# Two halves of the second MLP layer, laid between the strips of the first

## The chip, the cores and the metric

The kernel runs on one core of a Trainium2 chip. The metric is the device time of one execution in microseconds (us), as a median of runs. Before the change it is 2875.54 us over 3 runs (2875.34 to 2878.55).

## The reference

One layer of a hybrid encoder on 2048 prompt tokens and 64 sample tokens of width 1024: a normalised input projection into four head groups (one of them stick-breaking attention), an output projection, then an MLP of width 4096. Only the last part is touched:

```
x = x + g1 * mix
h2 = rmsnorm(x, ln2_g) * (1.0 + sc2) + sh2
x = x + g2 * (jnp.square(jax.nn.relu(h2 @ mlp_w1)) @ mlp_w2)
```

All of it is float32. The kernel splits each operand of a product into a high part, as TensorE's reduced float32 holds it, and a low remainder, and adds three products: high by high, low weight by high, high weight by low.

## The kernel before, in words

Everything that is transposed lies with features in the 128 partitions and tokens along the row. The last phase, `tail_phase`, takes the tokens in 4 blocks: 512 tokens in blocks 0 to 2, and 576 in block 3 (512 and the 64 sample tokens), which are done as two groups of 256 and 320 columns. For each block it does the output projection (`out`, 8 tiles) and a sum for the norm (`nsum`), and then the MLP in 16 chunks of 256 hidden features.

One chunk has two **strips** of the first layer (`hid`, ft = 0 and 1; 128 hidden features each). A strip is one accumulation of 24 matmuls (8 pieces of 128 input features, three products each; lines 2224, 2225, 2228). ScalarE reads the strip's PSUM bank (relu, L1890) and squares it into `g_hi` (L1892), VectorE squares it too and takes the remainder `g_lo` (L2075, L2077). Behind the strips of chunk c come the 8 **projection tiles** of chunk c-1 (`prj`, d = 0 to 7; lines 2266 to 2268): each multiplies both 128-feature parts of the preceding chunk's `g` by second-layer weights in 6 matmuls, and VectorE adds the tile into the residual `xs` (L2043). Chunk 0 has no projection tiles; the last two chunks of a block are projected together, later (`prj2`).

**Banks.** All these tiles use four PSUM banks in turn, `dn[u % 4]` for tile number u. TensorE waits in `bank(u)` until tile u-4 has been read out, by ScalarE for a strip and by VectorE for a projection tile.

**One order for all.** `walk` is a generator of the order of tiles. Each engine's program is written by one run of `walk` with its own callbacks, so all engines have the same order, and each engine's queue is strictly in that order. The order of weight loads comes from it too: `next_loads` says which weight strips are loaded behind which tile. Within a chunk these are four: the first-layer strips `w1` of the next chunk, one behind each `hid`, and the second-layer strips `w2` of this chunk, in a ring of four buffers, behind `prj` d = 3 and d = 7. Call them A and B (`w1`), C and D (`w2`). At chunk 0 there are no projection tiles, and the two `w2` strips are loaded behind the two `hid` tiles, behind A and behind B.

**What one load does.** In `load_for` SyncE's queue issues the load of the low part from a scratch in HBM (`load_lo`, L1629, blocks 1 to 3 only), then the load of the raw weights three places further on (`load_weights`, L1613 and L1616), for which it waits until ScalarE has converted the strip in hand (the raw buffers are three). ScalarE converts raw weights to the high part (`weights_hi`, L1756). In block 0 VectorE makes the low part (`weights_lo`, L1946), and it is stored to the scratch. A projection tile with d = 0 waits for both low parts of its `w2` (`lo_ready`).

**Attention in slots.** The attention of later blocks runs between these tiles. A strip takes 4 slots, a projection tile 1, so a chunk takes 16. Attention pair t starts at a fixed slot, `PRO + 43 * i // 4`, so a new pair comes every 10 or 11 slots. Its steps hang on that start: scores on TensorE, two sigmoids on ScalarE two slots later, VectorE's `scan` five slots later (two scans L1960, a copy, a product L1965), transposes and copies from 10 to 13, products with the values at 14 and 15. Each engine does the steps that are due before it goes on with its next tile, in its own queue.

In chunk 4 of blocks 1 to 3, `yt` puts one transposed output tile of the preceding block behind each projection tile; ScalarE copies it out (L1924). In chunk 1 GpSimd adds squares for the final norm (L1742), and in chunk 3 VectorE scales the finished block beside its other work.

Of the kernel before, what the change touches and what calls it, by code (L numbers as in the profile page):

```python
# [14 lines left out]
KT = D_MODEL // P  # L15
# [1280 lines left out]
def tail_phase(nc, const, x_v, o_v, q_v, k_v, sbv_p, sbv_s, cache_sb_v, w_out, mlp_w1, mlp_w2, y_prompt, y_sample):  # L1296
# [5 lines left out]
    NC = D_FF // P // 2  # L1302
# [4 lines left out]
    def groups(b):  # L1307

        return [(0, BLK)] if b < NB - 1 else [(0, HALF), (HALF, TMAX)]
# [43 lines left out]
    def walk(out, nsum, hid, prj, prj2, fsum, yt):  # L1353

        def opening(b):
            for f in range(KT):
                for g in range(len(groups(b))):
                    out(b, f, g)

        def sums(b):  # L1360
            for g in range(len(groups(b))):
                nsum(b, g)

        opening(0)
        sums(0)
        for b in range(NB):
            for c in range(NC):
                for ft in range(2):
                    for g in range(len(groups(b))):
                        hid(b, c, ft, g)  # L1370
                for d in range(KT if 1 <= c < NC - 1 else 0):
                    for g in range(len(groups(b))):
                        prj(b, c - 1, d, g)
                    if c == 4 and b:
                        yt(b - 1, d // 2, d % 2)
                if c == 2 and b:
                    fsum(b - 1, 0)
            if b + 1 < NB:
                opening(b + 1)
                for d in range(KT):  # L1380
                    prj2(b, d, 0)
                    if d == 0:
                        sums(b + 1)
        for g in range(len(groups(NB - 1))):
            for d in range(KT):
                prj2(NB - 1, d, g)
            for i in range(2 if g else 0):
                for v in range(2):
                    yt(NB - 1, i, v)
            fsum(NB - 1, g)  # L1390
        for i in range(2, TPB + 1):
            for v in range(2):
                yt(NB - 1, i, v)
# [7 lines left out]
    def count(kind, slots, by):  # L1401
        def one(*key):
# [10 lines left out]
        return one  # L1413

    walk(count("out", 4, PV), count("nsum", 0, PA), count("hid", 4, PA), count("prj", 1, PV), count("prj2", 2, PV),
         count("fsum", 0, PA), count("yt", 0, PA))
    for b in range(1, NB):
# [12 lines left out]
    def next_loads(kind, b, *key):  # L1430

        if kind == "start":
            return [("wo", 0, 0), ("wo", 0, 1)]
        if kind == "out":
            f = key[0]
            return [("wo", b, f + 2)] if f + 2 < KT else [("w1", b, 0, f + 2 - KT)]
        if kind == "hid":
            c, ft = key
            then = [("w1", b, c + 1, ft)] if c + 1 < NC else [("wo", b + 1, ft)] if b + 1 < NB else []
            return then + ([("w2", b, c, ft)] if c in (0, NC - 1) else [])  # L1440
        if kind == "prj":
            c, d = key
            return [("w2", b, c + 1, d // 4)] if d % 4 == 3 else []
        return []

    ring_no = {}
# [1 line left out]
    def count_loads(kind):  # L1448
        def one(b, *key):
            if key and key[-1] != last_group(b):  # L1450
                return
            for w in next_loads(kind, b, *key[:-1]):
                load_no[w] = len(load_no)
                ring = "w2" if w[0] == "w2" else "w1"
                ring_no[w] = sum((x[0] == "w2") == (ring == "w2") for x in load_no) - 1
        return one
# [3 lines left out]

    count_loads("start")(0)
    walk(count_loads("out"), nothing, count_loads("hid"), count_loads("prj"), nothing, nothing, nothing)
    load_list = list(load_no)
    ring_list = {False: [w for w in load_list if w[0] != "w2"], True: [w for w in load_list if w[0] == "w2"]}
# [56 lines left out]
    with ExitStack() as ctx:  # L1521
# [81 lines left out]
        def _(sp):  # L1603
# [85 lines left out]
            def load_for(kind):  # L1689
                def one(b, *key):  # L1690
                    u = tile_no[(kind, b, *key)]
                    slots.upto(slot_end[u])
                    if key[-1] != last_group(b):
                        return
                    for w in next_loads(kind, b, *key[:-1]):
                        if w[1]:
                            load_lo(w)
                        if load_no[w] + 3 < len(load_list):
                            load_weights(load_list[load_no[w] + 3])
                        if w[1] == 0:  # L1700
                            store_lo(w)
                    if kind == "hid" and key[0] == NC - 3 and key[1] == 0 and b + 1 < NB:
                        for i in range(6):
                            load_strip(b + 1, i)
                    if kind == "prj" and key[0] == 5 and key[1] == KT - 1 and 1 <= b and b + 1 < NB:
                        load_x(b + 1)
                return one
# [19 lines left out]
            for w in next_loads("start", 0):  # L1727
                load_weights(load_list[load_no[w] + 3])
                store_lo(w)
            walk(load_for("out"), nothing, load_for("hid"), load_for("prj"), nothing, nothing, store_rows)  # L1730
            for i in range(2):
                sp.wait_ge(y_out[i], 16 * (len(yt_no) // 2))
# [607 lines left out]
```

How the kernel before makes its waits and increments, by code:

```python
def wait(eng, sem, value):  # L57
    if not (isinstance(value, int) and value <= 0):
        eng.wait_ge(sem, value)
# [11 lines left out]
    def link(self, ins):  # L72
        self.n += 1
        ins.then_inc(self.sem, 1)
        self.eng.wait_ge(self.sem, self.base + self.n)
# [110 lines left out]
        @block.sync  # L186
# [16 lines left out]
            for c in range(1, NCH, 2):  # L203
                load_wada(sp, c)
                if c == 1:
                    load_rows(rows2, parts2, rows_in[1])
                    sp.dma_start(lra_raw[:, :].rearrange("p (k n) -> p k n", n=RANK),
                                 w_in[0].rearrange("(k p) n -> p k n", p=P)[:, :, OFF_LRA:OFF_LRA + RANK]
                                 ).then_inc(lra_in, 16)
                    for i in range(2):
                        sp.dma_start(mixc["wa2"][RANK * i:RANK * i + RANK, :], gla_wa2[0]).then_inc(blocks_in, 16)
                    sp.wait_ge(zeroed, 1)
                    for n in range(4):
                        for g, w in enumerate((rg_wa, rg_wx)):
                            sp.dma_start(mixc["rgw"][64 * (n % 2):64 * (n % 2) + 64, g, n // 2,
# [1 line left out]
                if c == 7:  # L218
                    for by in ("act", "dve"):
                        sp.wait_ge(tb_free[by], max(n for f in range(KT) for w, n in [turn_freed[turn_no["raw", f]]] if w == by))
                    sp.wait_ge(tb_free["act"], turn_freed[turn_no["raws", 0]][1])
# [2 lines left out]
            sp.wait_ge(blocks_in, 16 * 10)
            sp.wait_ge(raw_stored, 32)
```

## Time and profile before

| what | value |
|---|---|
| median of 3 runs | 2875.54 us (2875.34 to 2878.55) |
| profiled execution | 2876.38 us, its span 2874.6 us |
| granted TensorE clock, mean | 0.978 |
| TensorE matmul busy | 2744.9 us, 95% of the span |
| VectorE busy | 1466.1 us, 51% |
| ScalarE busy | 1273.9 us, 44% |
| DMA | 447.21 MB, mean 156 GB/s |

The span is the time from the first to the last instruction; the profiled execution's own time is 1.8 us longer. Times in rows are counted from the span's start. The `tail_phase` matmuls begin at about 768 us; block 0's output projection begins at 835 us, and the MLP strips of block 3 begin after 2420 us.

### The profile page before, as it was taken

The page shows a single profiled execution, that of the slowest core. Times are in us where ns is not written, and L with a number is a line of the kernel's source. Part 1 is how long each engine was busy: PE and PEld are TensorE (multiplying, and loading weights), DVE is VectorE, ACT ScalarE, POOL GpSimd, SP SyncE. Part 2 cuts the span into 40 slices and gives each one's busy share as a digit, 9 for nine tenths or more (in the row PEclk, how much of TensorE's full clock was granted, in tenths as well). Part 3 has the DMA queues.
Part 4 walks back from the last instruction along what each step waited for, and adds up shares of the span by engine and source line. Part 5 has one row for each costly group of instructions (what it writes and reads, how often), then busy time and mean ns, then how long its engine had stood idle before and what let it go on. Part 6 is the DMA issues. An engine that isn't in the chain of part 4 may idle for free.

```text
span 2874.6 us, 36899 instructions
## 1 busy us (share of the span) xinstructions
PE 2744.9 (95%) x14665; PEld 2243.1 (78%) x14665; DVE 1466.1 (51%) x2333; ACT 1273.9 (44%) x1949; POOL 35.1 (1%) x43
## 2 busy tenths in 40 slices
PE   7999999999878999999999999999999999999997
PEld 2589777777656777777877877777777789999996
DVE  4544554645335656575546455544555444545544
ACT  3375737455445343434444434445433443332233
POOL 0000000000000000000010000001000000100000
PEclk9999999999869999999999999999999999999999
DMA  9533353333524455555356555535555463555551
GB/s 328 174 103 111 103 160 110 111 114 91 192 81 156 148 150 164 162 176 187 118 166 196 175 162 187 183 95 176 183 187 161 154 226 117 194 163 165 176 166 51
DMA packets 381505, 447.21 MB, mean 156 GB/s; under 512 B 18716, under 2 KB 288983, under 8 KB 381335
## 3 DMA queue, kind: packets, MB, share of 16 engines
q1 hardware_dynamic: 375094, 432.26, 47.4%
q10 hardware_dynamic: 6240, 12.58, 1.2%
q8 instruction: 118, 1.93, 0.3%
q14 instruction: 53, 0.43, 0.0%
HBM read 374.00 MB, written 70.79 MB: 155 GB/s over the span
## 4 chain that ended last, share of the span: by engine, by line
PE 64%; DVE 4%; ACT 3%; DMA 1%; issue 1%; SPq 0%; DVEq 0%; ACTq 0%
PE t_dn L2224 11%; PE t_dn L2228 10%; PE t_dn L2225 10%; PE t_dn L2266 7%; PE t_dn L2268 6%; PE t_dn L2267 6%; PE t_ob L2170 4%; PE t_sc L2147 3%; PE t_wt L2159 2%; DVE t_left L1960 1%; PE t_dn L2289 1%; PE t_dn L2291 1%; PE t_dn L2290 1%; PE t_sc L2151 1%; DVE t_xs L2043 1%
## 5 line engine op out<-in xcount | busy, mean ns | idle before, releaser
L2224 PE MATMUL t_dn<-t_h_hi,t_w1h 128*128 128x512 f32 (+2 forms) x1600 | 589.2, 368 | 7.6 <-ACT t_h_hi L1872 3.1
L2043 DVE SCALAR_TENSOR_TENSOR t_xs<-t_dn,modT,t_xs 128x512 f32<-128x512 f32 (+2 forms) x768 | 422.7, 580 | 322.7 <-PE t_dn L2268 172.5
L2228 PE MATMUL t_dn<-t_h_lo,t_w1h 128*128 128x512 f32 (+2 forms) x1600 | 570.0, 356 | 2.3 <-DVE t_h_lo L2025 2.1
L2225 PE MATMUL t_dn<-t_h_hi,t_w1l 128*128 128x512 f32 (+2 forms) x1600 | 567.9, 355 | 0.0
L2266 PE MATMUL t_dn<-t_g_hi,t_w2h 128*128 128x512 f32 (+2 forms) x1120 | 412.4, 368 | 17.5 <-DVE t_xs L2043 15.3
L2268 PE MATMUL t_dn<-t_g_lo,t_w2h 128*128 128x512 f32 (+2 forms) x1120 | 397.6, 355 | 0.0
L2267 PE MATMUL t_dn<-t_g_hi,t_w2l 128*128 128x512 f32 (+2 forms) x1120 | 396.5, 354 | 0.0
L2075 DVE TENSOR_TENSOR t_rt<-t_rt 128x512 f32<-128x512 f32 (+2 forms) x160 | 95.9, 599 | 552.9 <-ACT t_g_hi L1892 552.9
L2224 PEld LDWEIGHTS t_dn<-t_h_hi,t_w1h 128*128 128x128 f32 x1600 | 305.2, 191 | 63.4 <-issue 27.4
L2228 PEld LDWEIGHTS t_dn<-t_h_lo,t_w1h 128*128 128x128 f32 x1600 | 304.1, 190 | 44.3 <-DVE t_h_lo L2025 3.2
L1890 ACT ACTIVATE t_rt<-t_dn 128x512 f32<-128x512 f32 (+2 forms) x160 | 83.7, 523 | 563.6 <-PE t_dn L2228 563.5
L2225 PEld LDWEIGHTS t_dn<-t_h_hi,t_w1l 128*128 128x128 f32 x1600 | 305.3, 191 | 31.7 <-issue 0.7
L1267 PE MATMUL f_zr<-hn_hi,f_w_hi 128*128 128x512 f32 (+1 forms) x880 | 321.4, 365 | 7.4 <-ACT f_gb L810 2.6
L1269 PE MATMUL f_zr<-hn_hi,f_w_lo 128*128 128x512 f32 (+1 forms) x880 | 314.0, 357 | 0.0
L1268 PE MATMUL f_zr<-hn_lo,f_w_hi 128*128 128x512 f32 (+1 forms) x880 | 312.7, 355 | 0.0
L2266 PEld LDWEIGHTS t_dn<-t_g_hi,t_w2h 128*128 128x128 f32 x1120 | 212.4, 190 | 60.4 <-DVE t_xs L2043 27.2
L1772 ACT ACTIVATE t_aT<-t_wt 128x512 f32<-128x512 f32 (+4 forms) x168 | 86.9, 517 | 368.4 <-PE t_wt L2159 368.3
L2268 PEld LDWEIGHTS t_dn<-t_g_lo,t_w2h 128*128 128x128 f32 x1120 | 212.1, 189 | 28.2
L2267 PEld LDWEIGHTS t_dn<-t_g_hi,t_w2l 128*128 128x128 f32 x1120 | 212.6, 190 | 21.0
L968 DVE TENSOR_TENSOR f_w_lo<-f_wraw,f_w_hi 128x1024 fp32r<-128x1024 f32 x88 | 107.7, 1224 | 214.3 <-ACT f_w_hi L777 214.1
L1960 DVE TENSOR_TENSOR_SCAN t_left<-t_left 128x512 f32<-128x512 f32 (+5 forms) x168 | 180.5, 1116 | 43.2 <-ACT t_taken L1765 40.6
L777 ACT ACTIVATE f_w_hi<-f_wraw 128x1024 fp32r<-128x1024 f32 x88 | 92.8, 1054 | 244.9 <-PE f_zr L1269 220.3
(312 smaller groups left out, 3662.8 us busy)
## 6 DMA issues: line engine op xcount, KB each, us to landing
t_raw<-in_mlp_w_dram SPq DMA_DIRECT2D x256, 512.0 KB, 4.5
t_w1l<-lo_scratch SPq DMA_DIRECT2D x120, 512.0 KB, 3.5
t_w2l<-lo_scratch SPq DMA_DIRECT2D x96, 512.0 KB, 5.6
f_wraw<-in_w_in_dram SPq DMA_DIRECT2D x88, 512.0 KB, 3.9
lo_scratch<-t_w1l SPq DMA_DIRECT2D x40, 512.0 KB, 5.3
t_raw<-in_w_out_dram SPq DMA_DIRECT2D x32, 512.0 KB, 5.1
lo_scratch<-t_w2l SPq DMA_DIRECT2D x32, 512.0 KB, 5.4
wada<-in_w_ada_dram ACTq DMA_DIRECT2D x6, 2048.0 KB, 12.6
```

Source lines behind the costliest of these rows:

```text
L1267: pe.matmul(out, wh, hi, start=(k == 0), stop=False)
L1268: pe.matmul(out, wh, lo, start=False, stop=False)
L1269: ins = pe.matmul(out, wl, hi, start=False, stop=(k == KT - 1))
L1960: ins = dve.tensor_tensor_scan(keep[:, j, ::-1], keep[:, j, ::-1], keep[:, j, ::-1], upto[:, j:j + 1], ALU.mult, ALU.min)
L2043: ins = dve.scalar_tensor_tensor(out=cols, in0=dn[u % 4][:, s - a:t - a], scalar=modT[:, mod + f, m:m + 1], in1=cols, op0=ALU.mult, op1=AL ...
L2170: ins = pe.matmul(ob[0:p.rows, at_col:at_col + HD], aT[0:p.kr, j, v * p.rows:(v + 1) * p.rows], vp[p.piece % 2][0:p.kr, v, HD * j:HD * j + ...
L2224: pe.matmul(out, hi[:, k, :], h_hi[:, k, a:e], start=(i == 0), stop=False)
L2225: pe.matmul(out, lo[:, k, :], h_hi[:, k, a:e], start=False, stop=False)
L2228: ins = pe.matmul(out, hi[:, k, :], h_lo[:, k, a:e], start=False, stop=(i == KT - 1))
L2266: pe.matmul(out[:, 0:e - a], hi[:, d, :], g_hi[c % 2][:, ft, a:e], start=(ft == 0), stop=False)
L2267: pe.matmul(out[:, 0:e - a], lo[:, d, :], g_hi[c % 2][:, ft, a:e], start=False, stop=False)
L2268: ins = pe.matmul(out[:, 0:e - a], hi[:, d, :], g_lo[c % 2][:, ft, a:e], start=False, stop=(ft == 1))
```

## The change

The 8 projection tiles no longer follow both strips: tiles d = 0 to 3 follow the first strip and tiles d = 4 to 7 the second. The loads of the two `w2` strips both come behind tile d = 7.

```
                 for ft in range(2):
                     for g in range(len(groups(b))):
                         hid(b, c, ft, g)
-                for d in range(KT if 1 <= c < NC - 1 else 0):
-                    for g in range(len(groups(b))):
-                        prj(b, c - 1, d, g)
-                    if c == 4 and b:
-                        yt(b - 1, d // 2, d % 2)
+                    for d in range(4 * ft, 4 * ft + 4 if 1 <= c < NC - 1 else 0):
+                        for g in range(len(groups(b))):
+                            prj(b, c - 1, d, g)
+                        if c == 4 and b:
+                            yt(b - 1, d // 2, d % 2)
...
         if kind == "prj":
             c, d = key
-            return [("w2", b, c + 1, d // 4)] if d % 4 == 3 else []
+            return [("w2", b, c + 1, ft) for ft in range(2)] if d == KT - 1 else []
```

In `next_loads`, c is the chunk that is projected, so c + 1 is the chunk in whose place the tile stands. A, B, C, D keep their order.

## Rows read from the trace of the kernel before

**Rows 1.** The page, part 1: engine, busy us, share of the span, instructions.
```profile
PE 2744.9 (95%) x14665; PEld 2243.1 (78%) x14665; DVE 1466.1 (51%) x2333; ACT 1273.9 (44%) x1949; POOL 35.1 (1%) x43
```

**Rows 2.** Waits of TensorE: who waited for whom, total us, times, longest.
```profile
PE t_dn L2266 <- DVE t_xs L2043: 15.3, 10, 2.4
...
PE t_dn L2266 <- ACT t_yrow L1924: 2.1, 1, 2.1
...
PE t_dn L2224 <- DVE t_xs L2043: 1.5, 1, 1.5
```

**Rows 3.** Timeline of VectorE, block 0, chunk 3: start, us, instruction, idle before it.
```profile
992.67 0.69 DVE L2075 TENSOR_TENSOR t_rt<-t_rt 128x512 f32<-128x512 f32 x1 [5.58 <-ACT t_g_hi L1892]
...
994.00 1.22 DVE L1946 TENSOR_TENSOR t_w1l<-t_raw,t_w1h 128x1024 fp32r<-128x1024 f32 x1
...
995.34 2.46 DVE L1960 TENSOR_TENSOR_SCAN t_left<-t_left 128x512 f32<-128x512 f32 x2
...
999.04 2.72 DVE L2043 SCALAR_TENSOR_TENSOR t_xs<-t_dn,modT,t_xs 128x512 f32<-128x512 f32 x4
```

**Rows 4.** Timeline of TensorE, block 0: chunk 3, first and fifth projection tile; chunk 13.
```profile
991.99 0.48 PE L2266 MATMUL t_dn<-t_g_hi,t_w2h 128*128 128x512 f32 x1
...
999.84 0.50 PE L2266 MATMUL t_dn<-t_g_hi,t_w2h 128*128 128x512 f32 x1 [2.16 <-DVE t_xs L2043]
...
1285.77 0.50 PE L2266 MATMUL t_dn<-t_g_hi,t_w2h 128*128 128x512 f32 x1 [0.55 <-DVE t_xs L2043]
```

**Rows 5.** Windows behind three stalls: engines' busy us (instructions), then clock, DMA share, GB/s.
```profile
940.50:943.90 3.40, 3.40 (x10) 2.65 (x9) 3.32 (x5) 0.00 (x0) 0.00 (x0) 0.51 0.69 240
1000.00:1003.40 3.40, 3.40 (x18) 2.81 (x19) 3.40 (x5) 0.07 (x1) 0.00 (x0) 1.00 0.08 28
1459.40:1462.80 3.40, 3.40 (x10) 2.53 (x9) 1.58 (x3) 1.52 (x3) 3.11 (x3) 0.50 0.37 112
```

**Rows 6.** Timelines of SyncE, chunk 0 of blocks 1 to 3: the second w2 low load.
```profile
1436.19 0.38 SPq L1629 DMA_DIRECT2D t_w2l<-lo_scratch  x1
...
1950.90 0.58 SPq L1629 DMA_DIRECT2D t_w2l<-lo_scratch  x1
...
2442.42 0.74 SPq L1629 DMA_DIRECT2D t_w2l<-lo_scratch  x1
```

**Rows 7.** DMA issues in those three instants: KB each, us from issue to landing.
```profile
t_w2l<-lo_scratch SPq DMA_DIRECT2D x1, 512.0 KB, 5.7
...
t_w2l<-lo_scratch SPq DMA_DIRECT2D x1, 512.0 KB, 5.3
...
t_w2l<-lo_scratch SPq DMA_DIRECT2D x1, 512.0 KB, 6.4
```

**Rows 8.** Timeline of TensorE, chunk 1 of blocks 1 to 3: around the second strip's start.
```profile
1438.34 0.39 PE L2228 MATMUL t_dn<-t_h_lo,t_w1h 128*128 128x512 f32 x1
1438.57 0.39 PE L2224 MATMUL t_dn<-t_h_hi,t_w1h 128*128 128x512 f32 x1
...
1953.98 0.39 PE L2224 MATMUL t_dn<-t_h_hi,t_w1h 128*128 128x512 f32 x1
...
2446.28 0.28 PE L2224 MATMUL t_dn<-t_h_hi,t_w1h 128*128 128x256 f32 x1
```

**Rows 9.** Timelines of VectorE and GpSimd in block 2, chunk 1.
```profile
1968.39 3.84 DVE L1960 TENSOR_TENSOR_SCAN t_left<-t_left 128x384 f32<-128x384 f32 x2
...
1965.37 11.40 POOL L1742 TENSOR_TENSOR t_st<-t_st 128x512 f32<-128x512 f32 x7 [502.36 <-ACT t_st L1831]
```

**Rows 10.** Block 3, chunk 7: first projection tile on TensorE, D's low load on SyncE; chunk 8.
```profile
2614.85 0.28 PE L2266 MATMUL t_dn<-t_g_hi,t_w2h 128*128 128x256 f32 x1
...
2618.76 1.35 SPq L1629 DMA_DIRECT2D t_w2l<-lo_scratch  x1
...
2640.45 0.28 PE L2266 MATMUL t_dn<-t_g_hi,t_w2h 128*128 128x256 f32 x1
```

**Rows 11.** DMA issues of that low load: KB each, us from issue to landing.
```profile
t_w2l<-lo_scratch SPq DMA_DIRECT2D x1, 512.0 KB, 7.1
```

## The prediction

> **What bounds the kernel now.** Part 1 of the page comes first: TensorE's matmuls are busy 95% of the span, every other engine about half [rows 1]. Nothing can be gained on another engine; what an order of tiles can move is TensorE's idle time, so the second view is TensorE's waits. Of those that hang on this order there are three [rows 2]: 15.3 us in 10 waits of projection tiles for VectorE's addition L2043 (a PSUM bank not yet read out), 1.5 us of one strip for the same, 2.1 us for ScalarE's copy of an output tile. The third view, the timelines around one such wait, shows how it arises. In chunk 3 of block 0 the second strip ends just before the first projection tile at 991.99 [rows 4]. VectorE works in its order: square and remainder of the strip from 992.67, a weight remainder at 994.00, then the attention scan that was due, from 995.34, and only at 999.04 the first tile's addition [rows 3]. The fifth tile needs that bank and starts at 999.84, printed as 2.16 us idle [rows 4]. The scan blocks 999.04 - 995.34 = 3.7 us.
>
> I counted from the code where scans fall in a chunk's 16 slots (0 to 3 and 4 to 7 the strips, 8 to 15 the tiles). A scan due in slot 8 or 9, right behind the strip, belongs to 8 of the 10 waits: block 0, chunks 1, 3, 5, 7 (slot 8), 11, 13 (slot 9), and block 2, chunks 8 and 10 (slot 8). The smallest is 0.55 us, in chunk 13 [rows 4]. Two more are in block 1, chunks 1 and 3, at slot 10 with GpSimd's or final-norm work beside it. The strip's 1.5 us is block 2, chunk 1, slot 12. A scan in a strip's slots runs beneath that strip and costs nothing.
>
> **Removed.** The waits printed are 15.3 + 1.5 + 2.1 = 18.9 us. A printed gap begins where the preceding matmul's modelled end is (0.39 us), while matmuls start 0.23 us apart [rows 8]; so each of the 12 is short by 0.16, and TensorE loses 18.9 + 12 x 0.16 = 20.8 us. Some stalls cost more: the granted clock behind the one at 940 was 0.51 for 3.4 us with 10 matmuls in it, behind the equally long one at 999.84 it was 1.00 with 18 [rows 5]. Of the five stalls of 2 us and more on this list three are followed by 3.4 us at the lower of the two clocks (1.2 instead of 2.4 GHz), which costs half of it, 1.7 us: 5.1 us. Together 25.9 us. In the new order scans of slots 8 to 11 lie beneath the second strip, so the slot-8 to slot-10 waits go. The copy of output tiles gets a strip's pause after four tiles, so its 2.1 us goes too; should that one stay, 2.3 + 1.7 us are lost again. What is late next are the two terms below.
>
> **Added 1: second-layer weights at chunk 1.** A projection tile needs both low parts of its weights. For chunk 0 the second is issued behind B, at 1436.19, 1950.90 and 2442.42 in blocks 1, 2 and 3 [rows 6], and takes 5.7, 5.3 and 6.4 us [rows 7]: landed at 1441.9, 1956.2, 2448.8. Before, two strips of chunk 1 cover this. Now the first projection tile stands where the second strip started, at 1438.57, 1953.98 and 2446.28 [rows 8], and everything up to there is as before. TensorE waits 3.3 + 2.2 + 2.5 = 8.0 us. Queued behind it on TensorE are the whole chunk and the attention steps. I take 8.0; it is below that only if landings get shorter (0 at 2.4 to 3.9 us), above if longer. In block 0 VectorE makes this remainder just in time, and I count 0.
>
> **Added 2: scans behind the new bursts.** A burst is now four tiles and then a strip. Only its first tile's bank comes due four tiles later with no strip in between (the next strip takes it); the banks of the other three come due behind that strip. So a scan in slots 5 or 13, where four and six of them fall now, costs nothing, and one in slots 4 or 12 costs what slot 8 cost. Four fall there: block 0, chunks 12 and 14 (slot 4), in the same place against the strip as the 999.84 case: 2.16 + 0.16 = 2.3 each [rows 4], 4.6. Block 2, chunks 1 and 3 (slot 12). In chunk 1 the scan meets GpSimd's adds: 3.84 us for two scans of 384 columns, while 7 adds fill 11.4 us beside it [rows 9], against 2.46 for two of 512 [rows 3]. Without GpSimd I put this stall at 0.7, with it at 2.8, and take 2.8, since four of the adds still follow the strip. Chunk 3 has value products on TensorE in between: 0.4. One scan in block 1, chunk 4, slot 5, lies in the burst with output tiles, where banks turn over twice as fast: 0.4. Sum 8.2; bounds 0 and 5 x 2.8 = 14.
>
> The GPSIMD Engine Reference of the Trainium skill (its table of specifications) says that GpSimd shares its SBUF interfaces with VectorE and contends with VectorE instructions that have two SBUF inputs, as the scan has. The trace's longer scan agrees; by that rule the 2.8 holds, without it the sum is 2.1 us lower.
>
> **Added 3: C and D in all other chunks.** Moving C to tile d = 7 moves four things: ScalarE's conversion of C now stands behind all attention steps up to slot 15; on SyncE the low load of C, then a raw load that waits for that conversion, then D's low load; in block 0 VectorE does both remainders in a row. From the end of the second strip to the tile that needs them there were 8 tiles and 2 strips, 2640.45 - 2614.85 = 25.6 us in block 3 [rows 10]; now 4 tiles and 1 strip, 12.8. D's low load was issued 2618.76 - 2614.85 = 3.9 us behind that strip [rows 10], as ScalarE does B, C, D in a row, and took 7.1 [rows 11]: 11.0, with 1.8 to spare. In blocks 1 and 2 attention lengthens both sides: where no step of ScalarE stands in slots 12 to 15 it is much the same; where one or two stand there the load goes out up to 4 us later, with a shorter queue of DMAs and more attention on TensorE, and I get between 0 and 1 us to spare. Late by my count are block 2, chunk 4 (about 1.3, output copies on ScalarE) and block 1, chunk 7 (about 1.7, an attention head's roots there). Bounds 0 and 0.5 us in each of 39 chunks, 20. I take half of 3.0 and 0.7 for the rest, 2.2, nearest to rows 10 and 11.
>
> **Added 4: the lower clock.** Of the new stalls six are over 2 us (three of added 1, two of block 0, one of block 2). At three in five and 1.7 us [rows 5]: 6.1; bounds 0 and 10.2.
>
> **Sum.** No instruction is added or taken away. Added 8.0 + 8.2 + 2.2 + 6.1 = 24.5, removed 25.9: -1.4 us. Against the profiled execution, 2876.4 us (span 2874.6 and 1.8 around it), that is 2875.0; the runs' median, 2875.5, is 0.9 lower, so 2874.1. I predict 2874.
>
> **Rivals.**
> *The bursts win (faster).* Shorter bursts let VectorE recover and the small terms vanish: added 1 stays (8.0), of added 2 the two in block 0 (4.6), added 3 is 0, the clock falls twice (3.4). 16.0 against 25.9: -9.9, so 2866. For it: the spare 1.8 us in block 3, and slots 5 and 13 free. Against it: the two scans with GpSimd and output tiles beside them. Chance 0.28.
>
> *Weights late in every chunk (slower).* D's low part becomes the bound in place of VectorE: its spare time is 1.8 us in block 3 and less elsewhere, so it decides from a landing of about 8.9 us, or an issue 1.8 us later. At 0.5 us in 39 chunks added 3 is 19.5 in place of 2.2, and the time is 2874 + 17 = 2891; at a third of the chunks 2880. For it: every low load stands behind a raw load and ScalarE's conversion. Against: in block 3 nothing but these weights uses ScalarE there. Chance 0.20, with what the clock may add.
>
> *It doesn't do what it says: a wait moves one tile on.* Scans behind the first strip stall as those behind the second did, and the removed 20.8 us comes back nearly whole in the second strips' bank waits: 8.0 more than before with added 1, 2883. Against it: the count of slots, four in place of eleven. It is part of the slower chance.
>
> **How the numbers follow.** 0.2% is 5.7 us, about what a measurement of this kernel can tell from no change. My case has 0.52 and falls within it; faster 0.28, slower 0.20. The range takes in the faster rival's 2866 and of the slower one the third of the chunks with some clock, 2886; my case's own range is 2870 to 2880.
>
> **What would show it.** Right: no waits of L2266 for VectorE in block 0 before chunk 12; one wait of L2266 for the DMA into `t_w2l` in chunk 1 of blocks 1, 2 and 3, of 2 to 3.5 us; strips L2224 waiting for L2043 in block 0, chunks 12 and 14; busy times as before. Wrong: waits for `t_w2l` in many chunks (the slower rival), or waits of strips for L2043 all over (the third); a time below 2868 with added 1 in the trace would mean that added 2 and 4 were too large.

## The result, and the profile after

The changed kernel takes 2885.23 us (median of 15 runs, 2881.99 to 2889.81); the kernel before, in turn with it, 2876.83 us (15 runs, 2871.84 to 2879.56). The ratio is 1.0029, with a 95% interval of 1.0021 to 1.0037: 8.4 us slower. The forecast was 2874, no change. The profiled execution of the changed kernel took 2888.46 us, 3.2 us more than its median; what follows is read from that one execution.

The page, part 1, of the changed kernel. It answers to [rows 1]; the span grew from 2874.6 to 2886.6 us.

```profile
span 2886.6 us, 36897 instructions
...
PE 2752.2 (95%) x14665; PEld 2249.4 (78%) x14665; DVE 1459.1 (51%) x2333; ACT 1274.3 (44%) x1949; POOL 33.2 (1%) x43
```

The instruction counts agree with those of before, so the difference is in waits and in the clock. Of the 12.0 us between the two spans 3.8 are there before the first MLP strip (it starts at 900.44 instead of 896.68 us), in code that the change doesn't touch; in the other kernels' traces it starts anywhere from 895.2 to 900.8 us. The other 8.2 us come behind it. That this is almost what lies between the medians is chance in part, for these are two single executions.

TensorE's waits after (who waited for whom, total us, times, longest) answer to [rows 2]:

```profile
PE t_dn L2266 <- DMA t_w2l<-lo_scratch: 16.2, 8, 4.6
...
PE t_dn L2224 <- DVE t_xs L2043: 7.9, 3, 3.6
...
PE t_dn L2224 <- DMA t_w1l<-lo_scratch: 3.1, 1, 3.1
...
PE t_dn L2266 <- DVE t_xs L2043: 0.8, 1, 0.8
```

The bank waits of projection tiles fell from 15.3 us in 10 to 0.8 in one. In their place stand 16.2 us in 8 waits for the low part of second-layer weights, which did not exist before. The single waits, from TensorE's timeline (start, us, instruction, idle before it):

```profile
1239.33 0.50 PE L2224 MATMUL t_dn<-t_h_hi,t_w1h 128*128 128x512 f32 x1 [2.16 <-DVE t_xs L2043]
...
1297.52 0.50 PE L2224 MATMUL t_dn<-t_h_hi,t_w1h 128*128 128x512 f32 x1 [2.16 <-DVE t_xs L2043]
...
1438.61 0.77 PE L2266 MATMUL t_dn<-t_g_hi,t_w2h 128*128 128x512 f32 x1 [4.62 <-DMA t_w2l<-lo_scratch]
...
1558.96 0.47 PE L2266 MATMUL t_dn<-t_g_hi,t_w2h 128*128 128x512 f32 x1 [1.10 <-DMA t_w2l<-lo_scratch]
...
1644.93 0.47 PE L2266 MATMUL t_dn<-t_g_hi,t_w2h 128*128 128x512 f32 x1 [0.96 <-DMA t_w2l<-lo_scratch]
...
1957.36 0.47 PE L2266 MATMUL t_dn<-t_g_hi,t_w2h 128*128 128x512 f32 x1 [2.40 <-DMA t_w2l<-lo_scratch]
...
1980.55 0.80 PE L2224 MATMUL t_dn<-t_h_hi,t_w1h 128*128 128x512 f32 x1 [3.61 <-DVE t_xs L2043]
...
2455.32 0.56 PE L2266 MATMUL t_dn<-t_g_hi,t_w2h 128*128 128x256 f32 x1 [3.70 <-DMA t_w2l<-lo_scratch]
...
2567.73 0.36 PE L2266 MATMUL t_dn<-t_g_hi,t_w2h 128*128 128x256 f32 x1 [2.07 <-DMA t_w2l<-lo_scratch]
```

The first two are block 0, chunks 12 and 14; the tiles at 1438.61, 1957.36 and 2455.32 are chunk 1 of blocks 1, 2 and 3; that at 1980.55 is the strip behind chunk 1's second burst; those at 1558.96 and 2567.73 are chunk 5, and 1644.93 is chunk 8. Two shorter ones for these weights (0.46 and 0.87 us) are in block 2, chunks 7 and 12; the tile of chunk 5 there waits 0.77 us, which the profile puts down to ScalarE (L1890).

The second `w2` low load of chunk 0, on SyncE's timeline in blocks 1 to 3 [rows 6], and its time from issue to landing (last number of the second list) [rows 7]:

```profile
1431.46 0.38 SPq L1629 DMA_DIRECT2D t_w2l<-lo_scratch  x1
...
1951.72 0.58 SPq L1629 DMA_DIRECT2D t_w2l<-lo_scratch  x1
...
2447.59 0.77 SPq L1629 DMA_DIRECT2D t_w2l<-lo_scratch  x1
```

```profile
t_w2l<-lo_scratch SPq DMA_DIRECT2D x1, 512.0 KB, 7.0
...
t_w2l<-lo_scratch SPq DMA_DIRECT2D x1, 512.0 KB, 5.5
...
t_w2l<-lo_scratch SPq DMA_DIRECT2D x1, 512.0 KB, 7.6
```

1431.46 + 7.0 = 1438.5, and the tile starts at 1438.61: TensorE waits for this landing and nothing else.

Windows behind four of the stalls, with columns as in [rows 5] (busy us and instructions of each engine, granted clock, DMA share, GB/s):

```profile
1438.70:1442.10 3.40, 3.40 (x10) 2.71 (x11) 0.48 (x1) 0.00 (x0) 0.00 (x0) 0.50 0.28 111
...
1980.60:1984.00 3.40, 3.40 (x8) 2.72 (x9) 1.87 (x3) 0.00 (x0) 0.36 (x1) 0.50 0.70 275
2455.40:2458.80 3.40, 3.40 (x15) 3.40 (x16) 0.71 (x2) 0.63 (x1) 3.07 (x3) 0.50 0.36 145
...
1297.60:1301.00 3.40, 3.40 (x17) 2.85 (x18) 1.84 (x3) 0.00 (x0) 0.00 (x0) 1.00 0.04 14
```

The three stalls over 3.5 us bring a stretch at 1.2 GHz (0.50), with 8 to 15 matmuls in these windows; that of 2.16 us before 1297.52 does not (1.00), nor do the others of this list, of 2.07, 2.16 and 2.40.

**The ledger.** I read off TensorE's timelines when each chunk starts in both traces, and took the steps of the difference (us). Where one chunk has several causes (block 1, chunk 1, say), its step is divided by the printed waits, 0.16 us added to each as in the prediction, and what remains is put down to the clock; so the sum is measured, its division in those chunks is a reckoning.

| term | predicted | found |
|---|---|---|
| removed, clock with it | -25.9 | -31.8 |
| added 1, weights at chunk 1 | 8.0 | 11.2 (4.8, 2.6, 3.9) |
| added 2, scans and output tiles | 8.2 | 10.1 |
| added 3, weights in other chunks | 2.2 | 9.0 |
| added 4, lower clock | 6.1 | 7.9 |
| block 1's first output tile | not named | 2.5 |
| last projection at the lower clock | not named | 1.5 |
| rest | 0 | -2.2 |
| sum | -1.4 | 8.2 |

### The profile page after: what moved, and what is told of

It is laid out like the page before. It is cut to its first block, busy times and chain, and to the rows that moved or that the text cites. A ratio compares the mean times of both kernels' runs of the same rounds, so it can differ in the third digit from the quotient of the medians.

```text
span 2886.6 us, 36897 instructions
## 1 busy us (share of the span) xinstructions
PE 2752.2 (95%) x14665; PEld 2249.4 (78%) x14665; DVE 1459.1 (51%) x2333; ACT 1274.3 (44%) x1949; POOL 33.2 (1%) x43
## 4 chain that ended last, share of the span: by engine, by line
PE 64%; DVE 3%; DMA 3%; ACT 2%; issue 1%; SPq 0%; DVEq 0%; ACTq 0%
PE t_dn L2224 10%; PE t_dn L2228 10%; PE t_dn L2225 10%; PE t_dn L2266 7%; PE t_dn L2268 7%; PE t_dn L2267 7%; PE t_ob L2170 4%; PE t_sc L2147 3%; PE t_wt L2159 2%; DMA t_w2l<-lo_scratch 2%; PE t_dn L2289 1%; PE t_dn L2291 1%; PE t_dn L2290 1%; PE t_sc L2151 1%; DVE t_left L1960 1%
## 5 line engine op out<-in xcount | busy, mean ns | idle before, releaser
L2266 PE MATMUL t_dn<-t_g_hi,t_w2h 128*128 128x512 f32 (+2 forms) x1120 | 412.2, 368 | 18.5 <-DMA t_w2l<-lo_scratch 16.2
L1890 ACT ACTIVATE t_rt<-t_dn 128x512 f32<-128x512 f32 (+2 forms) x160 | 83.7, 523 | 618.3 <-PE t_dn L2228 618.3
```

What stands on the lines that cost most here:

```text
L2266: pe.matmul(out[:, 0:e - a], hi[:, d, :], g_hi[c % 2][:, ft, a:e], start=(ft == 0), stop=False)
```

## The experiments

Two theories stood against each other. **Weights**: the order of tiles itself gains, and the loss is the low loads of `w2`, whose cover the new order halved. **Order**: the short bursts lose as much in bank waits and clock as the long ones did, and if the weights came earlier, other waits would take their place. In the diffs, lines with - are those of the changed kernel; the labels e1 to e10 are those that the expectations use. Line numbers in the profiles of these kernels are up to six higher than in the changed kernel. Where a kernel ran once, its time alone settles little (the kernel before ranged over 7.6 us in 11 runs beside these), and the waits and chunk lengths of its trace have to decide.

**Chunk 1 alone back (e1).** In chunk 1 of blocks 1 to 3 both strips run ahead of the 8 tiles again, with C and D at d = 3 and d = 7 there.

```
-                    for d in range(4 * ft, 4 * ft + 4 if 1 <= c < NC - 1 else 0):
+                    tiles = range(4 * ft, 4 * ft + 4) if split(b, c) else range(KT if ft else 0)
+                    for d in tiles if 1 <= c < NC - 1 else ():
```
with `split(b, c)` false for b > 0 and c = 1, and in `next_loads`, for a chunk that isn't split, the order of before.

> The changed kernel, but chunk 1 of blocks 1, 2 and 3 keeps the order of before (both strips, then eight tiles, C behind d = 3). Theory 'weights': the loss sits at chunk 1, where the first projection tile waits for the second low part of w2. In the trace of after, chunk 1 of blocks 1 to 3 and the slow clock behind it lengthen the way by 3.1, 7.4 and 6.4 us, 16.9 in all; undone, the time falls from 2885 to about 2868, and the waits of L2266 for the DMA into t_w2l in chunk 1 are gone. Rival 'bursts': the loss is in VectorE's scans behind the short bursts of all chunks; then little comes back, 2880 to 2885.

Measured: 2869.56 us (8 runs), ratio to before 0.9978 (0.9968 to 0.9988). The three chunks 1, of 56 chunks with projection tiles, carry the whole loss and more: without them the change is faster than the kernel before.

**The second w2 load of chunk 0 earlier (e2).** All tiles stay; the load goes ahead of B, one strip earlier.

```
+            if b and c == 0:
+                return then + [("w2", b, 0, i) for i in range(0 if ft else 2)]
             return then + ([("w2", b, c, ft)] if c in (0, NC - 1) else [])
```

> The changed kernel, but in chunk 0 of blocks 1 to 3 both w2 strips are loaded behind the first strip, ahead of B, instead of one behind each strip. The order of tiles is that of after. Theory 'weights': the three waits at chunk 1 (4.8, 2.6 and 3.9 us over the usual pitch in the trace of after) and the slow clock behind two of them (some 4.6 us) go, 15.8 in all: about 2869; the strip behind chunk 1 of block 2 still waits 3.8 for VectorE. Rival 'bursts': VectorE's waits take their place as soon as TensorE is no longer held there: 2880 to 2885.

Measured: 2870.36 us (9 runs), ratio 0.9975 (0.9965 to 0.9984). TensorE's waits in this kernel:

```profile
PE t_dn L2226 <- DVE t_xs L2045: 7.9, 3, 3.6
...
PE t_dn L2268 <- DMA t_w2l<-lo_scratch: 6.3, 4, 2.4
```

The waits for `t_w2l` fell by 16.2 - 6.3 = 9.9 us, and two of the three stalls that brought the lower clock went. These are about 9.9 + 2 x 2.5 = 14.9 us, as much as the medians differ (2885.23 - 2870.36 = 14.9). The agreement to a tenth is luck: the stall of 2.43 us in block 3, chunk 5, brought a stretch at 1.2 GHz here (0.50 from 2547.60 to 2550.90), and that of 2.07 us in the changed kernel did not. The bank waits did not grow. So the order of tiles need not be undone: an earlier load does the same.

**One half of the blocks each (e3, e4).** `split` is `b == 0` in the first kernel and `b > 0` in the second.

> The new order in block 0 alone, blocks 1 to 3 in the order of before (loads too). In block 0 VectorE makes the low parts and no load of them exists. Theory 'weights': block 0 keeps its gain, 11.1 us from the first strip to chunk 15 in the trace of after, less 2.5 at the first output tile of block 1, which waits for its low part there: 2877 - 8.5 = 2868. Rival 'bursts': short bursts cost in every block, so 2877 or more.

> The new order in blocks 1 to 3 alone, block 0 in the order of before. Theory 'weights': all the loss is here: from the start of block 1 to the end the trace of after is 16.7 us longer than that of before, so 2877 + 17 = 2894. Rival 'a loss spread over all blocks': no more than 2885.

Measured: block 0 alone 2868.27 us (6 runs), ratio 0.9972 (0.9960 to 0.9984); blocks 1 to 3 alone 2892.12 us (5 runs), ratio 1.0056 (1.0044 to 1.0069). The two differences to before, -8.4 and +15.4, add up to +7.0, near the change's +8.4. In block 0 the low weights are made on VectorE and don't come by DMA, and there the order gains; in blocks 1 to 3 they come by DMA, and there it loses. The list of waits of the second kernel has:

```profile
PE t_dn L2272 <- DMA t_w2l<-lo_scratch: 15.3, 9, 4.1
```

**The loads' move alone (e5).** All tiles in the order of before, C and D both behind d = 7 (`split` always false); one run.

> The order of tiles of before, with only the change of loads: C and D both behind tile d = 7. Theory 'weights': the move costs only when one strip, not two, covers it; here two do, so every chunk of blocks 1 to 3 takes what it takes in before, within 0.3 us, and the sum is within 2 us of before. Rival 'loads': moving C costs by itself; then waits for t_w2l in chunks 5 and 8 of blocks 1 to 3, as in after, some 8 us.

Measured: 2874.82 us, span 2873.0. With 8 tiles and 2 strips to cover them, no projection tile waits for `t_w2l`, and chunks 1 to 14 of blocks 1 and 2 agree with before within 0.3 us. Block 3 doesn't, against the expectation: its chunks 4 and 5 are 3.24 and 0.69 us shorter, for ScalarE's copy (L1924) is gone though no tile has moved. In block 0 chunk 4 is 1.37 us longer, and chunks 9 and 10 are 2.14 and 1.50 us shorter, as attention's wait of 1.85 us at the end of chunk 9 and the stretch at the lower clock behind it are gone. So 5.2 us of what the ledger calls removed (2.61, 1.13 and 1.46 in those chunks) come with the loads' move alone too; the tiles' order without it gives as much (2.66, 1.82 and 1.46 in e6, below), so either is enough. And block 1 begins 2.75 us later, for its first output tile waits for its own weights:

```profile
1335.08 0.47 PE L2228 MATMUL t_dn<-t_h_hi,t_w1h 128*128 128x512 f32 x1 [2.78 <-DMA t_w1l<-lo_scratch]
```

In the kernel before this wait was 0.95 us. Both low parts of chunk 14's `w2` in block 0 are now stored back to back (issued at 1317.40 and 1318.59 in the changed kernel), and block 1's first low load waits for all stores of weights loaded before its own. The second of them took 7.55 us and landed 13.5 us after chunk 15 began; in the kernel before it was stored alone, took 5.63 us and landed after 10.5. The price at block 1's start was 2.3 to 3.1 us in each of the eight kernels that load C and D together in block 0, and 0.0 to 0.1 in the three that do not.

**C back at d = 3 (e6).** The tiles of the changed kernel; one run.

```
-            return [("w2", b, c + 1, ft) for ft in range(2)] if d == KT - 1 else []
+            return [("w2", b, c + 1, d // 4)] if d % 4 == 3 else []
```

> The tile order of after, but C is loaded behind tile d = 3 as before (so ahead of B), D behind d = 7. Theory 'weights': D's low load is issued at once behind B, not behind the conversion of C, so the waits for t_w2l in chunks 5, 7 and 8 (about 8 us with the slow clock) fall to under 3; the three at chunk 1 stay, 8 to 11 us, for the loads of chunk 0 are the same. Rival 'order of tiles': they stay as in after.

Measured: 2877.96 us, span 2876.1. TensorE's waits for the weights:

```profile
PE t_dn L2266 <- DMA t_w2l<-lo_scratch: 9.4, 3, 4.0
```

All three are chunk 1. Chunk 5, whose weights are loaded among the output tiles of chunk 4, lost 1.34, 1.05 and 2.3 us in blocks 1 to 3 of the changed kernel and none here; chunk 8 of block 1 0.46 instead of 2.64. So 8.5 of the ledger's 9.0 us for added 3 came from C's place.

**GpSimd's adds made small (e7).** In chunk 1 GpSimd adds 16 of 512 columns of the squares; the rest of the final norm's sum is left out. One run.

```
-                pool.tensor_tensor(nacc[:, 0:n], nacc[:, 0:n], st[f % 2][:, 0:n], ALU.add).then_inc(n_acc, 1)
+                pool.tensor_tensor(nacc[:, 0:16], nacc[:, 0:16], st[f % 2][:, 0:16], ALU.add).then_inc(n_acc, 1)
```

> The changed kernel, but GpSimd's adds of squares in chunk 1 of blocks 1 to 3 take 16 columns instead of all (the rest of the sum for the final norm is left out). Theory 'GpSimd slows the scan': in block 2, chunk 1, the two scans of 384 columns fall from about 3.8 us to 1.9, the strip behind them waits under 2 us instead of 3.8, and the slow clock behind it goes: chunks 1 and 2 of block 2 shorter by 4 to 5 us. Rival 'the scan's place alone': unchanged.

Measured: 2879.73 us. Timelines of VectorE and GpSimd in block 2, chunk 1, first of the changed kernel, then of this one:

```profile
1973.85 4.04 DVE L1960 TENSOR_TENSOR_SCAN t_left<-t_left 128x384 f32<-128x384 f32 x2
...
1973.88 7.08 POOL L1742 TENSOR_TENSOR t_st<-t_st 128x512 f32<-128x512 f32 x4 [9.65 <-ACT t_st L1831]
```

```profile
1969.92 1.98 DVE L1960 TENSOR_TENSOR_SCAN t_left<-t_left 128x384 f32<-128x384 f32 x2
...
1970.48 1.43 POOL L1742 TENSOR_TENSOR t_st<-t_st 128x16 f32<-128x16 f32 x2 [0.30 <-ACT t_st L1831]
```

The same two scans take half as long when the adds beside them are short, and the strip behind them waits 0.67 us instead of 3.61:

```profile
1973.68 0.50 PE L2224 MATMUL t_dn<-t_h_hi,t_w1h 128*128 128x512 f32 x1 [0.67 <-DVE t_xs L2043]
```

The stretch at the lower clock behind that strip is gone. Chunks 1 and 2 of block 2 together cost 4.2 us less than in the changed kernel, although the wait of 2.15 us for the weights in chunk 1 brought such a stretch here (0.50 from 1953.30 to 1956.60).

**Every w2 pair early (e8).** Both `w2` strips of a chunk of blocks 1 to 3 are loaded behind that chunk's first strip, a whole chunk ahead of use.

```
+            if b and c < NC - 1:
+                return then + [("w2", b, c, i) for i in range(0 if ft else 2)]
...
-            return [("w2", b, c + 1, ft) for ft in range(2)] if d == KT - 1 else []
+            return [("w2", b, c + 1, ft) for ft in range(2)] if d == KT - 1 and not b else []
```

> The changed kernel, but in blocks 1 to 3 both w2 strips of every chunk (C and D) are loaded behind the first strip, behind A and ahead of B, instead of behind tile d = 7. Block 0 and the order of tiles as in after. Theory 'weights': the waits left in e2 for the DMA into t_w2l (6.3 us in 4 places, chunks 5, 7 and 8, with the slow clock some 8) go too, because D's low load is no longer queued on SyncE behind ScalarE's conversion of C and the attention steps before it: 2870 - 8 = 2862, and no wait of L2266 for t_w2l is left. Rival 'ScalarE': three conversions in a row behind the first strip delay ScalarE's relu and copies, and other waits take their place: 2870 or more.

Measured: 2867.99 us (6 runs), ratio 0.9967 (0.9955 to 0.9979). All waits for `t_w2l` by DMA are gone, but it is 6 us above what Weights expected. In block 3, chunk 4, a new wait of 5.0 us came, and this chunk is 3.73 us longer than before instead of 2.61 shorter, which is the 6 us. TensorE, ScalarE and SyncE there:

```profile
2525.47 0.38 PE L2226 MATMUL t_dn<-t_h_hi,t_w1h 128*128 128x256 f32 x1 [5.03 <-ACT t_yrow L1926]
```
```profile
2524.82 1.21 ACT L1926 ACTIVATE t_yrow<-t_dn 128x512 f32<-128x512 f32 x2 [8.27 <-DMA out_dram<-t_yrow]
```
```profile
2513.72 0.38 SPq L1618 DMA_DIRECT2D t_raw<-in_mlp_w_dram  x1
2514.15 0.58 SPq L1631 DMA_DIRECT2D t_w2l<-lo_scratch  x1
2514.77 0.44 SPq L1618 DMA_DIRECT2D t_raw<-in_mlp_w_dram  x1
2515.26 1.56 SPq L1631 DMA_DIRECT2D t_w2l<-lo_scratch  x1
2516.86 0.43 SPq L1615 DMA_DIRECT2D t_raw<-in_mlp_w_dram  x1
2517.34 9.05 SPq L1717 DMA_DIRECT2D out_dram<-t_yrow  x4
```

The stores of output rows stand behind the bunched weight loads on SyncE; ScalarE waits for them to land before it overwrites the row buffer, and TensorE for ScalarE. Here Order was right, in this one place.

**Both mends (e9, e10).** The early load of chunk 0 in blocks 1 to 3, and C at d = 3, D at d = 7, in the first kernel for blocks 1 to 3 and in the second for all blocks.

> The tile order of after. In blocks 1 to 3 both w2 strips of chunk 0 are loaded behind the first strip (as in e2), and in the other chunks C behind d = 3 and D behind d = 7 (as in e6); block 0 as in after. Theory 'weights': e6's chunk 1 prices (5.8, 3.4 and 5.1 us against e2's) go, and nothing waits for t_w2l any more; from the chunk times of e2 and e6 I get 16 us below before: about 2860. Rival 'something takes their place' (as the output copies did in chunk 4 of block 3 in e8): 2866 or more.

> As e9_both, but block 0 too loads C behind d = 3 and D behind d = 7. In e6 that made chunk 12 of block 0 cost 1.6 us more than in after and the first output tile of block 1 2.3 to 3.1 us less. Theory: the two cancel, within 2 us of e9_both; block 0's place for C is no part of the loss. Rival: block 0's loads matter as those of blocks 1 to 3 do, 5 us or more between the two.

Measured: 2861.02 us (5 runs), ratio 0.9944 (0.9932 to 0.9957), and 2859.73 us (5 runs), ratio 0.9943 (0.9929 to 0.9956). Both beat the changed kernel, and the one before by 0.56 and 0.57%; between the two the medians can't tell. Counted from the start of chunk 15, block 1's first output tile comes 0.11 us later than before in the second and 3.08 later in the first. Neither kernel's list has a wait for `t_w2l` by DMA; the largest of this case's stalls that are left in the first are the strips' bank waits and block 1's first loads, which in the second wait 2.8 us, 1.5 at most, as in the kernel before (2.9, 1.8 at most):

```profile
PE t_dn L2228 <- DVE t_xs L2047: 7.9, 3, 3.6
...
PE t_dn L2228 <- DMA t_w1l<-lo_scratch: 3.9, 3, 3.1
```

The second expectation came true on the medians, but not for its reason. The 1.6 us that chunk 12 of block 0 cost more in e6 were not the price of C's place: in e10, with C in the same place and the same stall of 2.16 us, the chunk took what it takes in the changed kernel (2.48 and 2.47 us more than before). The windows behind this stall, first of e6, then of e10:

```profile
1239.15:1242.55 3.40, 3.40 (x8) 2.72 (x9) 3.03 (x4) 0.00 (x0) 0.00 (x0) 0.50 0.50 173
```
```profile
1234.10:1237.50 3.40, 3.40 (x18) 2.68 (x18) 3.00 (x4) 0.00 (x0) 0.00 (x0) 1.00 0.48 162
```

In the two profiled executions nothing cancels: from the first strip to block 1 the second kernel is 3.6 us shorter than the first. The medians differ by 1.3 us only, so what block 0's place for C is worth stays open.

In the first kernel's trace blocks 1 and 3, from their first strip on, are 5.1 and 3.6 us shorter than before, so with its loads mended the order gains there too; block 2 is 0.3 us longer, for the strip behind the scan beside GpSimd's adds still waits 3.6 us.

So Weights held: it told the sign and, within 2 us, the size of six of the seven timed kernels. It missed by 6 us the one with every pair early, where Order's new wait came.

## Why the prediction was wrong, step by step

The time, 2885, lies outside the forecast case's own 2870 to 2880. The wider range, 2866 to 2886, took it in only through what it allowed the slower rival, and, as shown below, not for that rival's reason: that was luck.

**What bounds the kernel**: right. What the change moves is TensorE's idle time, and busy times of the other engines hardly changed.

**Removed**: right in kind, too small. The listed waits of block 0, chunks 1 to 13, came off with 11.8 us together, and the clock behind one of them. 4.2 us in its chunks 4, 9 and 10 were not counted: attention's own waits on TensorE (`t_wt` for VectorE and ScalarE), whose three largest rows fell from 28.0 to 23.7 us in the whole list, and the clock behind one of them. Block 1, chunk 1, gave 4.1 (seen bare in the last kernel, where this chunk is 4.00 us shorter than before), and chunk 3 2.7; the copy of output tiles gave 2.6 in block 3, though not by the order of tiles alone: e5 shows that the loads' move is enough for it, and for chunks 9 and 10 of block 0. One sign of being right failed in a small way: a projection tile of block 0 did wait for VectorE before chunk 12, not for an addition but for the remainder that VectorE makes of C and D in a row, which had no price:

```profile
1148.83 0.47 PE L2266 MATMUL t_dn<-t_g_hi,t_w2h 128*128 128x512 f32 x1 [0.60 <-DVE t_w2l L1946]
```

**Added 1** failed in its size. The place, the wait and its releaser are as forecast. I took landings of 5.7, 5.3 and 6.4 us from one execution [rows 7] and made them a point; after the change they took 7.0, 5.5 and 7.6, although the load went out as long after the chunk's first matmul as before (1431.46 - 1428.39 = 3.1 us in block 1, 1436.19 - 1433.13 before). Each microsecond of landing went straight onto the path. It cost 11.2 us instead of 8.0, and two of the three stalls were long ones that brought the lower clock. The 11.2 are the top of what the runs show: in e4, e6 and e7, whose chunks 0 and 1 of blocks 1 to 3 have the same tiles and loads, the three waits come to 8.6, 9.8 and 9.3 us by the same count.

**Added 2** was near. Chunks 12 and 14 of block 0 cost 2.47 and 2.46 us (forecast 2.3), block 2, chunk 3, 0.33 (0.4). The scan with GpSimd beside it cost 3.8 instead of 2.8, and the output tiles of block 1, chunk 4, 1.10 instead of 0.4. GpSimd's part in it, argued before, is now shown by the run with small adds. The GPSIMD Engine Reference of the Trainium skill (section 1, Specifications) says that GpSimd shares its SBUF interfaces with VectorE, with contention for VectorE instructions that have two SBUF inputs; 4.04 us beside long adds and 1.98 beside short ones agree with it.

**Added 3** is the step that failed most: 9.0 us instead of 2.2. I had found both late places by the count of slots (the weights loaded in block 2, chunk 4, and block 1, chunk 7) and then took half of them, drawn to block 3's spare 1.8 us [rows 10, 11]. And I counted chunk 4 for block 2 alone, though output tiles stand in chunk 4 of all three blocks. SyncE's and ScalarE's timelines in block 1 of the changed kernel show the queue:

```profile
1550.38 0.33 SPq L1715 DMA_DIRECT2D out_dram<-t_yrow  x1
...
1551.32 0.39 SPq L1616 DMA_DIRECT2D t_raw<-in_mlp_w_dram  x1
1551.76 0.58 SPq L1629 DMA_DIRECT2D t_w2l<-lo_scratch  x1
```
```profile
1550.25 2.00 ACT L1756 ACTIVATE t_w2h<-t_raw 128x1024 fp32r<-128x1024 f32 x2
```

D's low load goes out at 1551.76: SyncE has to put the raw load at 1551.32 ahead of it, which waits for the first of ScalarE's two conversions, begun at 1550.25, and these stand behind the output tiles' copies. It took 7.1 us, so it landed at 1558.8, and the tile started at 1558.96. The slower rival named this mechanism, weights late beyond chunk 1, but in 13 to 39 chunks; they were late in six. So neither the forecast nor the rival told it rightly: most chunks kept their spare time, and six cost 0.7 to 2.6 us each. That more work on ScalarE makes those late is shown for chunk 4's loads by the rows above, and only argued for the other three places.

**Added 4**: the count was off one way, the price the other. Three stalls of the terms above brought 1.2 GHz instead of "three in five" of six, but each cost about 2.6 us and not 1.7, as the lower clock lasted until 1443.5, 1986.3 and 2460.7, 4.9 to 5.7 us beyond the end of the stall and not 3.4.

**Not named at all**: the stores at the end of block 0 that block 1's first low load waits for, 2.5 us: a wait of 3.10 us and a stretch at the lower clock behind it, less the shorter waits that stood there before. The prediction counted the queue past which the loads moved, and not what waits for the stores that they bring.

**The third rival**, a wait that moves one tile on, did not come: bank waits fell from 15.3 + 1.5 to 0.8 + 7.9 us.

Of the 9.6 us between forecast and ledger (8.2 + 1.4), added 3 is 6.8, added 1 3.2, block 1's start 2.5, added 2 and the clock 3.7 together, and the last projection's clock 1.5; removed gave 5.9 back and small steps 2.2. So the step that failed is the cover of the second-layer weights: in added 3, where the lateness counted for two chunks was halved and the output tiles of two blocks were left out, and in added 1, where a single landing was taken as sure; beside it stand the stores of block 0, which had no term.

## What to carry to other kernels

When an interleaving brings a consumer forward, list every load that the old order covered and its spare time, place by place, and set a bound by the longest landing that the trace has for such a load, beside the one in that place. Look for the mend before judging the order: here the same order lost 0.3% with its loads as they came and gained 0.6% with one of them a strip earlier and another where it had been. Loads that are moved take their queue with them: what they wait for, what is stored behind them, and the output rows that stand behind them on the same engine.

## What the runs showed that was not expected

- One and the same load, at the same place of the program, took 5.7 us from issue to landing in one execution and 7.0 in another (block 1), 6.4 and 7.6 (block 3), while the chunks of block 0, where TensorE waits for no DMA, are the same within 0.1 us in the kernel before and in e4, which leaves that block alone. Over eight kernels the load in block 1 took 5.6 to 6.0 us in the four with the old order in chunk 1 (before, e1, e3, e5) and 6.0 to 7.0 in the four with the new one (after, e4, e6, e7); in block 3 it was 5.9 to 6.6 and 6.0 to 7.6. The loads issued just before and behind it are the same, so whether the order has a part in the longer landings stays open.
- Two scans of 384 columns took 1.98 us beside short GpSimd adds and 4.04 beside long ones: a factor of two for VectorE from an engine that is busy 1% of the span.
- The length of a stall doesn't tell whether the lower clock comes. From block 0's chunk 1 on, the stalls of 3.1 us and more in the changed kernel brought it, the four of 2.07 to 2.40 in the chunks did not; before, three of five at 2 to 2.4 us did. The windows of e6 and e10 above show one and the same stall with both outcomes. So does the last projection, with a stall of 2.23 us in both kernels. TensorE's timeline and the window behind it, of before:

```profile
2822.04 0.36 PE L2289 MATMUL t_dn<-t_g_hi,t_w2h 128*128 128x256 f32 x1 [2.23 <-DVE t_g_lo L2077]
...
2822.30:2825.50 3.20, 3.20 (x29) 3.20 (x29) 0.79 (x2) 0.42 (x1) 0.00 (x0) 1.00 0.00 0
```

and of after, 29 matmuls against 16 in 3.2 us (the 1.5 us of the ledger's line on the last projection):

```profile
2832.77 0.54 PE L2289 MATMUL t_dn<-t_g_hi,t_w2h 128*128 128x256 f32 x1 [2.23 <-DVE t_g_lo L2077]
...
2833.00:2836.20 3.20, 3.20 (x16) 3.20 (x17) 0.43 (x1) 0.00 (x0) 0.00 (x0) 0.50 0.00 0
```
